# Layer 0's expert opening: dense tiles routed first, the fetched tile last, no rows summed in it

## The reference

```
q = (ub @ P['peer_wq']).reshape(t, PEER_HEADS, 2, PEER_QDIM // 2)
s = jnp.einsum('thpd,pkd->thpk', q, P['peer_subkeys'])
sv, si = lax.top_k(s, PEER_TOPK)
cand = (sv[:, :, 0, :, None] + sv[:, :, 1, None, :]).reshape(t, PEER_HEADS, PEER_TOPK * PEER_TOPK)
top, ci = lax.top_k(cand, PEER_TOPK)
e = si0[ci // PEER_TOPK] * PEER_NKEYS + si1[ci % PEER_TOPK]
gate = jax.nn.softmax(top, axis=-1)
act = gelu(einsum('tkd,td->tk', P['peer_u'][e], ub))
return einsum('tk,tkd->td', gate * act, P['peer_v'][e])
```

## Time and profile before

| | us |
|---|---|
| median of 3 runs | 5634.15 |
| lowest and highest | 5629.9, 5634.39 |
| the profiled execution, device time | 5625.92 |
| its span, first to last instruction | 5624.1 |

### The profile page before, as it was taken

The page is one execution under the profiler, slowest core; times in us unless marked ns, Lnnn a source line. Parts: engine busy times, 40 slices in busy tenths (PEclk is TensorE's granted clock), DMA queues, the critical chain, the costliest instruction groups (busy, mean ns, idle before and its releaser), DMA issues.

```text
span 5624.1 us, 63951 instructions
## 1 busy us (share of the span) xinstructions
PE 5117.2 (91%) x22762; PEld 3358.4 (60%) x22762; DVE 3608.3 (64%) x8028; ACT 1396.9 (25%) x3522; POOL 1555.8 (28%) x1540
## 2 busy tenths in 40 slices
PE   8999989999778999999999799989988669999997
PEld 4788565648645555555554488855666546666665
DVE  3554456546787888886776555454556877766666
ACT  1110133222574121121112211023222561111111
POOL 0000000000136666565553000000000255545552
PEclk9999899999889999999999899999889889999999
DMA  4000003314248999999997100001314279999997
GB/s 145 5 12 9 23 16 105 102 57 172 99 172 337 420 413 417 411 417 415 412 420 318 52 9 9 8 23 49 101 46 142 91 266 417 419 417 411 417 412 289
DMA packets 294093, 1191.38 MB, mean 212 GB/s; under 512 B 24848, under 2 KB 107024, under 8 KB 208272
## 3 DMA queue, kind: packets, MB, share of 16 engines
q0 software_dynamic: 92160, 671.13, 28.9%
q1 hardware_dynamic: 195856, 460.83, 22.5%
q10 hardware_dynamic: 5760, 55.33, 2.4%
HBM read 1135.81 MB, written 51.38 MB: 211 GB/s over the span
## 4 chain that ended last, share of the span: by engine, by line
PE 65%; DVE 15%; DMA 13%; ACT 3%; issue 2%; POOL 1%; ACTq 0%; DVEq 0%; SPq 0%; POOLq 0%
PE psum L546 65%; DMA arena<-in_ut 10%; DVE arena L1593 2%; DMA arena<-gate_blocks 1%; DVE arena L2078 1%; DVE arena L1996 1%; DMA x_tokens<-in_uv,arena 1%; DVE arena L1797 1%; DVE arena L1602 1%; DMA arena<-in_uv,arena 1%; DVE arena L1795 1%; DVE y_features L1876 1%; DVE y_features L1904 1%; DVE x_tokens L1602 1%; DVE arena L1596 1%
## 5 line engine op out<-in xcount | busy, mean ns | idle before, releaser
L546 PE MATMUL psum<-arena 128*128 128x64 f32 (+4 forms) x8128 | 1381.6, 335 | 39.5 <-DVE arena L1996 23.9
L546 PE MATMUL psum<-u_features,weight_ring 128*128 128x256 f32 (+2 forms) x4672 | 1352.9, 441 | 12.1 <-DVE u_features L1599 6.1
L546 PEld LDWEIGHTS psum<-arena 128*128 128x128 f32 (+1 forms) x8128 | 979.2, 196 | 407.9 <-issue 302.1
L546 PEld LDWEIGHTS psum<-u_features,weight_ring 128*128 128x128 f32 x4672 | 882.2, 193 | 375.8 <-issue 179.7
L546 PE MATMUL psum<-u_features,arena 128*128 128x384 f32 (+1 forms) x2048 | 598.4, 448 | 63.9 <-DMA arena<-in_ut 56.4
L1565 POOL TENSOR_TENSOR arena<-consts 128x1 f32<-128x1 f32 x640 | 353.5, 552 | 1070.5 <-DVE y_features L1904 929.9
L546 PE MATMUL psum<-weight_ring,consts 128*128 128x512 f32 x1280 | 573.3, 595 | 5.1 <-DVE consts L1891 5.1
L546 PEld LDWEIGHTS psum<-u_features,arena 128*128 128x128 f32 x2048 | 402.5, 198 | 284.4 <-DMA arena<-in_ut 80.4
L1301 ACT ACTIVATE arena<-arena 128x1 f32<-128x1 f32 x640 | 129.8, 203 | 1763.6 <-DVE arena L1896 1762.0
L1566 POOL DMA_INDIRECT arena<-in_uv,arena x358 | 539.4, 1507 | 101.7 <-POOL arena L1565 95.6
L1896 DVE CUSTOM_DVE_ANT_0 arena<-arena,y_features 128x1024 f32<-128x1024 f32 x358 | 437.1, 1221 | 73.5 <-DMA arena<-in_uv,arena 72.8
(11 more groups left out here) (215 smaller groups left out, 5215.6 us busy)
## 6 DMA issues: line engine op xcount, KB each, us to landing
weight_ring<-in_ws SPq DMA_DIRECT2D x242, 512.0 KB, 3.5
weight_ring<-in_ut SPq DMA_DIRECT2D x128, 512.0 KB
weight_ring<-in_uv SPq DMA_DIRECT2D x128, 512.0 KB
arena<-in_ut SPq DMA_DIRECT2D x128, 512.0 KB
arena<-in_uv SPq DMA_DIRECT2D x128, 512.0 KB
gate_blocks<-arena ACTq DMA_DIRECT2D x20, 2048.0 KB, 7.1
arena<-gate_blocks SPq DMA_DIRECT2D x32, 768.0 KB, 35.8
arena<-gate_blocks SPq DMA_DIRECT2D x32, 512.0 KB, 29.5
```

What stands on the lines that cost most here:

```text
L546: return pe.matmul(o, w, x, start=first, stop=last, skip_group_check=True)
```

## The change

Only where a layer has three query parts, which is layer 0, does the planner do anything new:

- Routing goes through the dense tiles first, and then through the first fetched tile.
- The first turn is not listed ahead of the end of the second query part. The 16 pieces of the third part no longer stand among the first 32 groups, but among the other 64, one ahead of each fourth group.
- No slot is put into the opening. The first four fetches keep their place behind the first half of the fetched tile's routing.
- Tiles 0 to 3 lie in score buffers 3, 1, 0, 2 instead of 0, 1, 2, 3, since tiles 4 and 5 take over buffers 0 and 1, which must be those of tiles routed early.
- SP waits, in both layers, for the first fetched tile to be routed too before it loads blocks 2 and 3.

```diff
-SCORES_IN = ({0: 0, 1: 1, 2: 2, 3: 3, 4: 0, 5: 1}, {2: 0, 3: 1, 4: 2, 5: 0})
+SCORES_IN = ({0: 3, 1: 1, 2: 0, 3: 2, 4: 0, 5: 1}, {2: 0, 3: 1, 4: 2, 5: 0})
...
-            order = [FETCHED[l][0]] + list(DENSE[l])
+            three = len(QUERIED[l]) > 2
+            order = list(DENSE[l]) + [FETCHED[l][0]] if three else [FETCHED[l][0]] + list(DENSE[l])
+            apart = (len(DENSE[l]) - 1) * GROUPS // WQ
...
-                    events.append((now, "turn", gates // GROUPS, 0))
-                    ready = now + 2.5
+                    at0 = max(now, piece_at(1, WQ)) if three else now
+                    events.append((at0, "turn", gates // GROUPS, 0))
+                    ready = at0 + 2.5
                 if ready is not None and ready <= now:
-                    if gates < GROUPS and gates % 2 == 0 and len(QUERIED[l]) > 2:
-                        events.append((ready, "piece", 2, gates // 2))
-                        events.append((ready + 6.9, "kept", 2, gates // 2))
-                        if gates == GROUPS - 2:
-                            events.append((ready + 7.6, "tail", 2, WQ - 1))
-                        ready += 0.8
+                    if three and gates >= GROUPS and gates % apart == 0:
+                        c = (gates - GROUPS) // apart
+                        events.append((ready, "piece", 2, c))
+                        events.append((ready + 6.9, "kept", 2, c))
+                        if c == WQ - 1:
+                            events.append((ready + 7.6, "tail", 2, c))
+                        ready += 1.4
...
-                    if r == 0 and i == HALF - 1:
+                    if order[r] == FETCHED[l][0] and i == HALF - 1:
                         fetches = [(now + 0.5 + 1.3 * n, "fetch", n, 0) for n in range(len(EARLY_RING))]
-                    if r >= 2 and i % 7 == 6:
+                    if r >= 2 and i % 7 == 6 and not three:
                         events.append((now, "slot", slots, 0))
                         slots, now = slots + 1, now + 2.7
-                elif gates < len(DENSE[l]) * GROUPS - 1:
+                elif gates < len(DENSE[l]) * GROUPS - 1 and not three:
                     events.append((now, "slot", slots, 0))
                     slots, now = slots + 1, now + 2.8
...
                 sp.wait_ge(*at("routed", l, DENSE[l][-1]))
+                sp.wait_ge(*at("routed", l, FETCHED[l][0]))
                 for m in range(2, 4):
```

## The result

The changed kernel took 5585.77 us (median of 4 runs, 5573.65 to 5595.5) where the kernel before took 5632.02 (4 runs) beside it: ratio 0.9916, 95% interval 0.9902 to 0.993. A second timing gave 0.9925 (0.9912 to 0.9939). So it is faster by 42 to 47 us by the two ratios; forecast was 18, and the range's lower end, 5590, was missed by 4.

A forecast was written before the change was run, and what follows sets the result against it. The prediction took VectorE's routing and TensorE to bound most of layer 0's opening, and TensorE and DMA together its loop. Opening -76, entry 0 and loop +58 summed to -18 us: 5616 as a median, range 5590 to 5641.

The forecast's parts named there:

- The likeliest case: Whole kernel: opening gains 76 us, layer 0's loop pays 58, so -18 us; chance 0.66.
- What bounds the opening: Layer 0's opening: TensorE waits for VectorE's routing, then TensorE bounds the first third, VectorE the second; late routing delays the last.
- The opening, -76: Layer 0, up to the last gate group: it comes at 1671 instead of 1747.1, 76 us earlier; bounds -91 and -58.
- With three engines that near each other I add 5 us: Opening's second third: TensorE's floor 86 us, VectorE about 78, ScalarE about 79; 5 us added, 91 us forecast.
- The entry: Last gate group to first weighting in layer 0: late weight blocks cost zero, 10 us if all came late.
- The loop, +58: Layer 0's expert loop: 25 more slots, 26.2 MB, cost 63 us at 416 GB/s, less 5 for a fuller ramp.
- is bound twice: Layer 0's loop before: TensorE busy 1251.6 of 1254 us, and DMA engines also full at 416 GB/s.
- The range: Whole time 5590 to 5641 us, taking in the main case (-42 to +5) and the even one.
- Against the median: Whole time: profiled execution 5625.92 us, 8.2 below the median 5634.15; forecast 5608 against it, 5616 as a median.
- DMA has room: Rival, layer 0's loop: DMA only keeps TensorE's pace, 25 slots cost 0 to 25 us, total 5571; chance 0.10.
- The pieces set the pace: Rival, opening's two later thirds: 8 pieces drag every group, thirds cost 24 and 27 us more, total 5667; chance 0.11.
- The planner's pitch: Rival, opening: groups take the planner's 2.7 us each, opening -58 and loop +58 cancel, total 5634; chance 0.13.

The follow-up runs named there:

- the run without slots: Kernel before with the 25 slots of layer 0's opening moved into the loop, old order kept: 5638.42 us, ratio 1.0014.
- with 15 slots: Changed kernel with the planner's routing part at 2.0 us instead of 2.45 and 15 slots back in the last third: 5591.01 us, ratio 0.9931.
- 6 KB layout: Gate matrix laid out in HBM by chunk for 6 KB reads in layer 0: changed kernel 5568.1 us, ratio 0.9884; kernel before 5600.46 us, 0.9942.

## Why the prediction was wrong

The mechanism and the sign were right, the size was not: -18 was forecast, -42 to -47 came. The likeliest case happened, and none of the rivals did; its terms were sized wrongly, nearly all in the same direction.

- *What bounds the opening*: right, stage by stage. First transposes at once after the pieces, no late routing, thirds of 69.5, 86.8 and 85.7 us.
- *The opening, -76*: it was -90. The step that failed is the margin laid on top of the floors: 5.5 us in the first third, 4.2 and 2.3 in the others; 2.5 more were saved ahead of the first lane. "With three engines that near each other I add 5 us" was not needed: the thirds with pieces ran on TensorE's floor of 86 (86.8, 85.7). In the first third I took 75 from the present second third's 71.6, pricing its two slots at 5 us; the run without slots took 64.5 with two parts more, so that with the prediction's own 4 us for these parts the two slots were worth some 11, and the third came to 69.5. The floors had been written down as the bound, -91, and came within 1 us. That is partly luck: the joins took 5.3 and 5.4 and not 3, which the early first lane and a first third 1.5 under its 71 made good.
- *The entry*, 0: right, -2.1. The late weight blocks delayed nothing.
- *The loop, +58*: it was +48.8. The rows' own price held: 63 us less the 5 for a fuller ramp was 58, and on DMA alone the moved slots cost 58.6. The step that failed is to add it whole to a loop that "is bound twice". Through the loop the two limits are level, as it says, and the changed kernel reached its 125th weighting (at 3016.12) 55.8 us later in its loop (1333.4 against 1277.6). But the kernel before ended 8.9 us above its time with half of TensorE's product (1302.4 against 1293.5), all of it on the last three blocks, and with 384 slots TensorE's time no longer counts: 58.6 - 8.9 = 49.7. 48.8 lies within the prediction's bounds of +42 and +68, nearer to the lower one.
- *The range* let one term reach its bound while the other goes half way. Both went far: -90 + 48.8 = -41, just inside its -42. The entry (-2.1) and the rest of the span (-2.5), for which it had nothing on the fast side, and a kernel before that ran 2.1 faster in this timing than the median on which the forecast stood, took the time out of it.
- *Against the median*: the profiled execution of the kernel before stood 8.2 us below its median, that of the changed kernel 2 above. 6.1 of these 10 us are the stretch ahead of the expert stage.
- *DMA has room* was wrong: with half of TensorE's product the changed kernel's loop stayed at 1352 us, at 416 GB/s. The 435 GB/s of the Trainium skill ("Perfetto Trace Analysis", section "Roofline") appear in no run here; with the large gate loads it was 421 and 422.
- *The pieces set the pace* needed both later thirds over 104 us; they took 86. *The planner's pitch* needed 2.7 us a group; the first third ran at 2.2.

## What to carry to other kernels

When engines are ordered by hand and each has a floor in a stage, forecast the largest floor, not the floor with an allowance, and keep the allowance for the range. In this case that held where only parts, pieces and groups meet; with 15 slots the last third took 99.9 us where its fullest engine was busy 90.8. Work moved into a stage costs the difference between the new largest floor and the old largest floor. Where another engine sets that stage today, even if only at its end, its margin over the one that gets the work comes off the price, and cutting the other engine's work by half in one run measures that margin. Compare two profiles from the first instruction that differs, or the part before it is counted as the change's.

## What was not expected of the hardware

- The DMA share read 1.00 at 396 GB/s and 1.02 at 414 to 417: here the share didn't tell how much is left, the rate did.
- With the 6 KB layout, which stores the gates in 512 B runs instead of whole rows of a partition, the thirds in which rows are fetched and summed were shorter. Layer 1's last third, in the changed kernel and then with the layout:

```profile
L1881 DVE TENSOR_TENSOR y_features<-psum,consts x32: 676/681/693, 4483.9 to 4570.6; 128x512 f32<-128x512 f32 x32
```

```profile
L1886 DVE TENSOR_TENSOR y_features<-psum,consts x32: 676/681/692, 4482.4 to 4562.4; 128x512 f32<-128x512 f32 x32
```

86.7 us became 80.0; in the kernel before, layer 0's last third went from 88.9 to 81.5 and layer 1's from 86.6 to 80.6. That the fetches then wait less behind a store is likely, but no run here separates it from the layout's other effects.
